# The last gate by TensorE with two more rows, in quarters; last embeddings in the row loop; last row scaled by VectorE

## The reference

```python
ffn = peer(x, peer_wq, peer_subkeys, peer_u, peer_v)    # 8 heads x 16 experts a position
x = layer_norm(DEEPNORM_ALPHA * x + ffn, ln2_g, ln2_b)
gate = sigmoid(x @ ple_wgate + ple_bgate)               # 1024 -> 1024
ple = gate * (p @ ple_wproj)                            # 256 -> 1024
x = layer_norm(DEEPNORM_ALPHA * x + ple, ln3_g, ln3_b)

def peer(x, w_q, sub_keys, u_tab, v_tab):
    q = (x @ w_q).reshape(B, S, 8, 2, 128)
    scores = einsum('bshpk,hpnk->bshpn', q, sub_keys)
    # top 16 of each half, top 16 of their 256 sums -> expert ids, softmax -> gates
    h = einsum('thkd,td->thk', u_tab[ids], x)
    act = gates * gelu(h)
    return einsum('thk,thkd->td', act, v_tab[ids])
```

## Time and profile before

| | us |
|---|---|
| median of 3 runs (lowest, highest) | 1508.1 (1507.87, 1511.52) |
| the profiled execution, its own time | 1511.14 |
| its span, first to last instruction | 1509.1 |
| busy: PE, DVE, ACT, POOL | 1156.4, 1071.6, 926.1, 587.5 |
| DMA in the chain that ended last | 32% |
| bytes moved, mean rate | 595.55 MB, 395 GB/s |

### The profile page before, as it was taken

How to read it: one execution, slowest core, us unless ns; L and a number is a source line. 1 busy time by engine, 2 the same in 40 slices (tenths; PEclk the granted TensorE clock), 3 DMA queues, 4 the chain that set the end, 5 groups by cost and what they waited for, 6 DMA issues and landing times.

```text
span 1509.1 us, 19032 instructions
## 1 busy us (share of the span) xinstructions
PE 1156.4 (77%) x6928; PEld 917.1 (61%) x6928; DVE 1071.6 (71%) x2604; ACT 926.1 (61%) x1577; POOL 587.5 (39%) x528
## 2 busy tenths in 40 slices
PE   8989999988666986777568977878566666677766
PEld 6556776666665775666546756555456665666553
DVE  0467776658777786778566666778976677789875
ACT  1136675667767787776556567665566666666561
POOL 1024444334444344344433444444345444534330
PEclk9999999989989999899777897999787777888898
DMA  9559999999999999999999999999999999999990
GB/s 370 208 232 421 421 420 422 420 421 421 421 421 421 394 394 422 421 421 420 424 421 421 399 421 422 419 422 420 402 422 421 420 421 420 422 379 404 407 387 21
DMA packets 84807, 595.55 MB, mean 395 GB/s; under 512 B 9445, under 2 KB 12005, under 8 KB 14826
## 3 DMA queue, kind: packets, MB, share of 16 engines
q0 software_dynamic: 73728, 536.90, 86.1%
q1 hardware_dynamic: 10986, 57.44, 9.4%
HBM read 592.21 MB, written 2.10 MB: 394 GB/s over the span
## 4 chain that ended last, share of the span: by engine, by line
DMA 32%; PE 24%; DVE 23%; ACT 11%; issue 5%; POOL 4%; SPq 0%; ACTq 0%; DVEq 0%
DMA arena<-in_uv,ids 32%; PE ps L844 10%; DVE arena L1251 9%; PE ps L634 4%; ACT arena L1008 4%; POOL arena L468 4%; PE ps L777 2%; PE ps L611 2%; PE ps L493 2%; PE ps L486 2%; ACT actv L1003 2%; DVE cands L1191 1%; DVE cands L1192 1%; DVE pick L1193 1%; PE ps L698 1%
## 5 line engine op out<-in xcount | busy, mean ns | idle before, releaser
L468 POOL DMA_INDIRECT arena<-in_uv,ids x512 | 582.4, 1137 | 834.3 <-PE ps L844 710.1
L844 PE MATMUL ps<-ident,arena 128*128 128x128 f32 x4096 | 631.9, 315 | 325.0 <-ACT arena L1008 323.6
L1251 DVE CUSTOM_DVE_ANT_0 arena<-arena 128x1024 f32<-128x1024 f32 x512 | 619.0, 1224 | 308.4 <-DMA arena<-in_uv,ids 301.2
L844 PEld LDWEIGHTS ps<-ident,arena 128*128 128x128 f32 x4096 | 549.4, 163 | 433.8 <-ACT arena L1008 395.0
L1008 ACT ACTIVATE arena<-arena,actv 128x1024 f32<-128x1024 f32 x512 | 556.9, 1135 | 0.0
L1000 ACT ACTIVATE gel<-hid 128x2 f32<-128x2 f32 x256 | 51.9, 203 | 448.3 <-DVE hid L1251 441.8
L634 PE MATMUL ps<-arena 128*128 128x128 f32 x1024 | 127.5, 286 | 0.8 <-ACT arena L934 0.8
L1003 ACT ACTIVATE actv<-gel,gates 128x1 f32<-128x1 f32 x512 | 122.9, 287 | 8.4
L634 PEld LDWEIGHTS ps<-arena 128*128 128x128 f32 x1024 | 126.0, 204 | 1.5 <-issue 1.5
L698 PE MATMUL ps<-arena 128*128 128x384 f32 x192 | 65.9, 486 | 0.0
L611 PE MATMUL ps<-arena 128*128 128x512 f32 x128 | 59.4, 610 | 1.1 <-DVE arena L1120 1.1
(11 more groups left out here) (141 smaller groups left out, 923.0 us busy)
## 6 DMA issues: line engine op xcount, KB each, us to landing
arena<-in_wq SPq DMA_DIRECT2D x22, 1024.0 KB
arena<-in_w_out SPq DMA_DIRECT2D x4, 2048.0 KB, 16.1
arena<-in_uv,ids POOLq DMA_INDIRECT x512
arena<-in_w_gate SPq DMA_DIRECT2D x1, 4096.0 KB, 17.9
arena<-in_w_k SPq DMA_DIRECT2D x4, 512.0 KB, 6.4
arena<-in_w_q SPq DMA_DIRECT2D x2, 1024.0 KB, 10.7
arena<-in_w_gv SPq DMA_DIRECT2D x1, 2048.0 KB, 16.1
arena<-in_w_v SPq DMA_DIRECT2D x1, 2048.0 KB, 21.6
```

The lines of the kernel that those rows point to most:

```text
L468: nc.gpsimd.indirect_dma_start(out=rows[:, c % RING, :], out_offset=None, in_=a["uv"][:, :], in_offset=bass.IndirectOffsetOnAxis(ap=ids[:, ...
L844: i = mm(ps[:, run_bank(r) + k // 4, (k % 4) * P:(k % 4 + 1) * P], rows[:, c % RING, D + k * P:D + (k + 1) * P], ident[:, :], is_transpose ...
L1251: v.tensor_tensor_reduce(out=r, in0=r, in1=x1[t], scale=1.0, scalar=0.0, op0=ALU.mult, op1=ALU.add, accum_out=hid[:, i, c:c + 1]).then_inc ...
```

## The change

The gate of a tile becomes sigmoid(rstd * (y @ W' - mu * sum(W') + sd * bias')), with sd = (var + eps) * rstd. The two corrections are one more matmul with two rows of weights (-mu and sd, `fixT`) against two rows (sum(W') and bias', `fix_rows`), accumulated onto the gate product. ACT reads PSUM and applies rstd as the sigmoid's scale, and `open_gate` goes. In detail:

- the two rows come from one set of matmuls with 2-column weights at steps 133 to 140; the 16 matmuls of the second set, a copy of 1024 columns and the addition of the bias go; one gain less is spread; the columns of gains are made at step 130 instead of 131, the gate weights scaled from 144 instead of 143;
- tile 0's tail begins at step 156 instead of 164;
- in a tail, PE transposes the two values at b+4 and adds the correction at b+7; sigmoids at b+8 instead of b+10; second embeddings at b+9 instead of b+8; DVE multiplies and adds at b+9 and b+11; variance at b+12 and norm at b+13, one step earlier;
- tile 3's embeddings run at step 250 in the loop;
- the last gathered row is scaled by DVE and not by ACT;
- tile 3's gate is made in four quarters of 256 columns.

```diff
-TAIL_AT = {0: 164, 2: 225, 1: 240}
+TAIL_AT = {0: 156, 2: 225, 1: 240}
-SPREAD_AT, COLUMNS_AT, BIAS_AT, SCALE_AT, MEAN_AT = 120, 131, 134, 143, 152
+SPREAD_AT, COLUMNS_AT, SUMS_AT, SCALE_AT = 120, 130, 133, 144
...
                 for k in range(k0, k0 + 2):
-                    w = neg_one[:, :] if i else gcols[:, KD + k:KD + k + 1].to_broadcast([P, P])
-                    m = mm(ps[:, 4 + j, :], w, w_gate[:, k, j * HALF:(j + 1) * HALF],
...
+                    mm(ps[0:2, 4 + j, :], gcols[:, k, :], w_gate[:, k, j * HALF:(j + 1) * HALF],
+                       start=(k == 0), stop=False, skip_group_check=True)
...
+            def transpose_fix(i, bank):
+
+                pe.wait_ge(fix_ready, i + 1)
+                if bank == 5:
+                    pe.wait_ge(y_read, i + 1)
+                nc.tensor.transpose(ps[0:2, bank, 0:P], fix[:, :], ident[:, :]).then_inc(fix_tr, 1)
+
+            def gate_fix(i, c0, c1, bank, place=0):
+
+                pe.wait_ge(fixT_ready, i + 1)
+                mm(ps[:, bank, place:place + c1 - c0], fixT[:, :], fix_rows[:, c0:c1], start=False, stop=True,
+                   skip_group_check=True).then_inc(gate_done, 1)
...
                     if step == b + 7:
+                        gate_fix(i, 0, HALF, 6)
+                        gate_fix(i, HALF, D, 4)
                         embedding_product(i, 0, 5)
-                    if step == b + 8:
-                        pe.wait_ge(gate_in, 2 * i + 1)
+                    if step == b + 9:
+                        pe.wait_ge(gate_ready, 2 * i + 1)
                         embedding_product(i, 1, 6)
+                if step == NU * NG - 6:
+                    pe.wait_ge(run_added, NR - 1)
+                    for j in range(2):
+                        embedding_product(NT - 1, j, 2 - run_bank(NR - 1) + j)
...
             y_transposes(last)
             pe.wait_ge(score_used, NU)
-            for j in range(2):
-                gate_product(last, j, 0, KD, 6 + j)
+            for c in range(4):
+                gate_product(last, c * QD, (c + 1) * QD, 0, KD, (6, 7, 4, 5)[c])
+                if c == 0:
+                    transpose_fix(last, run_bank(NR - 1))
+                else:
+                    gate_fix(last, (c - 1) * QD, c * QD, (6, 7, 4)[c - 1])
+            gate_fix(last, 3 * QD, D, 5)
...
+            def gate_sigmoid(i, n, c0, c1, bank):
+
+                act.wait_ge(gate_done, 2 * i + n + 1)
+                fn(gate[:, c0:c1], ps[:, bank, 0:c1 - c0], ACT.Sigmoid, scale=rstd[:, 0:1]).then_inc(gate_ready, 1)
...
+                if step == SUMS_AT + KD + 1:
+                    keep_sums()
                 for i in range(NT - 1):
                     b = TAIL_AT[TAILS[i]]
-                    if step == b + 10:
-                        gate_sigmoid(i, 0)
-                        gate_sigmoid(i, 1)
+                    if step == b + 6:
+                        keep_fix(i, 5)
+                    if step == b + 8:
+                        gate_sigmoid(i, 0, 0, HALF, 6)
+                        gate_sigmoid(i, 1, HALF, D, 4)
...
+            v.tensor_scalar(r, r, actv[:, (NU - 1) % 4, c:c + 1], None, ALU.mult).then_inc(last_scaled, 1)
             add_run(NR - 1)
```

More of the change, by code:

```diff
@@ L146, in build @@
         gG = sb("gG", [P, WB])
-        gcols = sb("gcols", [P, 2 * KD])
+        gcols = sb("gcols", [P, KD, 2])
         gaggr = sb("gaggr", [P, 2, 2])
         grstd = sb("grstd", [P, 2])
-        murs = sb("murs", [P, 1])
-        stats = sb("stats", [P, 2, 6])
+        fix = sb("fix", [P, 2])
+        fixT = sb("fixT", [2, P])
+        stats = sb("stats", [P, 4, 6])
         aggr = sb("aggr", [P, 2])
@@ L841, in combine @@
                     pe.wait_ge(run_added, r if r < 3 else r - 1)
-                pe.wait_ge(scaled, u * TOPK + c + 1)
+                if u * TOPK + c + 1 < NU * TOPK:
+                    pe.wait_ge(scaled, u * TOPK + c + 1)
+                else:
+                    pe.wait_ge(last_scaled, 1)
                 for k in range(KD):
@@ L1059, in _ @@
             last = NT - 1
-            gate_sigmoid(last, 0)
-            gate_sigmoid(last, 1)
+            keep_fix(last, run_bank(NR - 1))
+            for c in range(4):
+                gate_sigmoid(last, c, c * QD, (c + 1) * QD, (6, 7, 4, 5)[c])
         @block.vector
@@ L1317, in y_var @@
                 mean_var()
-                step(v.tensor_tensor(murs[:, :], aggr[:, 0:1], rstd[:, :], ALU.mult))
+                v.tensor_scalar(fix[:, 0:1], aggr[:, 0:1], -1.0, None, ALU.mult)
+                v.tensor_tensor(fix[:, 1:2], var_e[:, 0:1], rstd[:, 0:1], ALU.mult).then_inc(fix_ready, 1)
             def y_centre(i):
@@ L1328, in y_rescale, with add_embedding @@
                                             op0=ALU.mult, op1=ALU.add))
[L1330 to L1347 removed]
+            def add_embedding(i, n, c0, c1, bank, place, chunk):
+                part = gate[:, c0:c1]
+                dst = x2[TAILS[i]][:, c0:c1]
+                dve.wait_ge(gate_ready, 2 * i + n + 1)
+                if i < NT - 1:
+                    dve.wait_ge(embedding_done, 2 * i + n + 1)
+                else:
+                    dve.wait_ge(embedding_done, 2 * NT)
+                v.tensor_tensor(part, ps[:, bank, place:place + c1 - c0], part, ALU.mult).then_inc(ple_used, 1)
+                dve.wait_ge(ple_used, 2 * i + n + 1)
+                step(v.scalar_tensor_tensor(out=dst, in0=dst, scalar=ALPHA, in1=part, op0=ALU.mult, op1=ALU.add))
+                half_stats(dst, chunk)
             def background(at_step):
@@ L1421, in _ @@
             free = 2 - run_bank(NR - 1)
+            c = TOPK - 1
+            r = rows[:, c % RING, D:2 * D]
+            dve.wait_ge(actv_ready, NU * TOPK)
+            v.tensor_scalar(r, r, actv[:, (NU - 1) % 4, c:c + 1], None, ALU.mult).then_inc(last_scaled, 1)
             add_run(NR - 1)
@@ L1426, in _ @@
             y_rescale(last)
-            for j in range(2):
-                open_gate(last, j, 6 + j)
-                if j == 0:
-                    add_embedding(last, 0, free)
-            add_embedding(last, 1, free + 1)
-            mean_var()
+            for c in range(4):
+                add_embedding(last, c, c * QD, (c + 1) * QD, free + c // 2, c % 2 * QD, c)
+            mean_var(4)
             normed_halves(x2[TAILS[last]], ln3_g, ln3_b, out_ready)
```

131 lines of the change are left out of this document (51 added, 80 removed).

## The result

| | before | after |
|---|---|---|
| median of 6 runs (lowest, highest), us | 1508.8 (1507.87, 1511.52) | 1513.9 (1512.9, 1516.07) |
| ratio, 95% interval | | 1.0027 [1.0015, 1.004] |
| profiled execution, its span, clock | 1511.14, 1509.1, 0.878 | 1513.33, 1511.3, 0.879 |
| last dots end, last variance starts | 1472.92, 1501.14 | 1474.24, 1503.26 |

The kernel became 0.27% slower (4.1 us by the ratio of the runs side by side, 5.1 between the medians). By the bound of 0.3% this is no change, but it is outside the predicted range (1500 to 1510) and of the wrong sign. So the medians say how much, and the traces only where.

The account below looks back on a forecast made before the run. The stream of row gathers was taken to bound the loop, then the chain behind the last gather. Loop +0.2 and end -2.9 gave -2.7 us: 1508.4 profiled, 3.0 lower as median, 1505.4; range 1500 to 1510 (8 in 10).

Parts of the forecast that it names:

- Tile 2's tail: In the loop: PE's added matmuls and ACT's wait, less VectorE's lighter steps, cost +1.1 us; ends 0 and +4.5.
- Columns: In the loop: gain columns one step earlier, away from the query, win back 1.0 of the dip's 2.0 us.
- Tile 0's tail: In the loop, 8 steps earlier: VectorE's fewer, spread instructions give -0.6 of 1.6 us; ends -1.6 and +0.5.
- Dots: At the end: tile 1's norm moves out of the way of the last dots, -0.3 of 2.9 us.
- Last row by DVE: At the end: VectorE scales one row while ACT scales the other; -0.5 us taken, ends 0 and -1.1.
- Embeddings: At the end: 4.39 us leave the chain, but PE waits 0.7 for the last addition; net -3.7 us.
- Clock: At the end: the 8 transposes and 0.2 us of gate product now fall in the half-clock stretch, +1.0 us.
- Gate in quarters: Last tile's gate: 0.4 us wait for fix values, 0.1 small transpose, 1.72 for four fix matmuls; together +2.2 us.
- Behind PE: From PE's end to the last variance: 2.8 us where it was 4.51, -1.7; ends -1.2 and -1.9.
- ACT and PE hold each other up: Slower rival, tails of tiles 2 and 1: sigmoids waiting for PE block rows PE needs; 10.1 us in all, 1515.3; 13%.
- The clock stays low: Second rival, at the end: PE's idling misses the clock's rise, half speed under the gate product, +1.7 us, 1507.1; 17%.
- The fast rival: In the loop: the dips close, loop -3.0 us, with the end's -4.5 the time is 1500.6; 20%.

Follow-up runs that it names:

- e12: The changed kernel without the correction of the gate in any of the four tiles; ratio to the kernel before 0.9979.
- e10: The kernel before with columns at step 130, last embeddings at step 250, gate in quarters, last row by DVE, correction still by DVE; ratio 0.9982.
- e11: The changed kernel without the correction in the loop (tiles 0, 2 and 1), the last tile keeping it; ratio to the kernel before 0.9996.
- e7: The kernel before with only the last gathered row scaled by DVE; ratio to the kernel before 0.9993.
- e3: The kernel before with only the last tile's embeddings moved to step 250; ratio to the kernel before 0.9984.
- e1: The changed kernel with the last tile's embeddings again behind the loop; ratio to the kernel before 1.0029.
- e5: The changed kernel without the correction in the last tile; ratio to the kernel before 1.0001.
- e4: The changed kernel with three unused matmuls on PE ahead of the last step's rows; ratio to the kernel before 1.0006.
- e2: The changed kernel with the loop's sigmoids and what follows them later, last embeddings at step 252, PE's correction kept; ratio to the kernel before 1.0023.
- e8: The kernel before with only the columns of gains at step 130 instead of 131; ratio to the kernel before 0.9992.

## Why the prediction was wrong, step by step

**The step that failed** is the pricing of the correction by PE. It had three terms: +1.1 for tile 2's tail, +0.7 for tile 1's, and +2.2 for quarters and fix matmuls, 4.0 together, against -6.7 for all else. The runs put it at 7.2 us (the changed kernel against e12), and all else at -3.2 (e12 against the kernel before; e10 gives -2.7). Both halves were off: the cost by 3.2, the gains by 3.5. The correction's matmuls take 8.2 us of PE in the changed kernel's trace, three times 1.91 in the loop (from their start to that of the embeddings) and four times 0.62 at the end. I let the queue of gathers cover most of the loop's part and took none for tile 0; the runs charge it almost at its full length on PE.

- *Tile 2's tail*: ACT's wait was predicted at about 4.5 us with the table load in it, on the right rows, and it was 3.54 behind the load. The consequence was wrong. I wrote that "0.5 us is felt", because PE comes late too. But the region 1312 to 1384 lost 6.7 us where it had lost 5.0, +1.7, inside the ends of 0 and +4.5. That is about a quarter of the price I gave the rival in which PE and ACT hold each other up (2.7 of 10.1, with tile 1's tail). With tile 1's tail (3.7 lost, before 2.7: +1.0, predicted +0.7) the late tails cost 2.7 in the trace, predicted 1.8. The ratio of e11 says 4.7 us, give or take 2.5, for all three tails.
- *Columns*: the dip went wholly, better than the 1.0 taken, but the distance to the query, the reason given, is not what these traces show: the 32 matmuls ran mostly at full clock, 4.24 us and not 6.98. *Tile 0's tail*: its dip at 1060 went too. But neither gave a microsecond to the whole. Between 700 and 1312 seven kernels with the old loop lost 3.8 to 5.2 us, seven with the changed one 2.7 to 5.9. In place of the 1.9 us before 904 stand 2.3 us behind 1120 (in stretches the change does not touch), and in place of the dip at 1060 the one at 976. The predicted -1.6 was about 0: the step took a local repair for a gain. Why the later dips come is not settled.
- *Dots*: their end came 1.3 us later, at 1474.24, not 0.3 earlier. The last gather landed at 1472.99; I had worked out 1471.4 from the old landing. That is a part of the 2.7 us that the loop's windows lost more.
- *Last row by DVE*: 0.75 us for 1024 columns, not the 1.3 taken from the nearest row, and ready before ACT's row at 1476.03. The 16 transposes gave none of it back, as they ran at 1.2 GHz throughout (3.69). e7 alone measured -0.07 points (1 us), with an interval that includes both 0 and the predicted 0.5.
- *Embeddings*: the loop hid them, as predicted, except for a start of the next rows 1.8 us later. In the old kernel the move brings 0.16 points (e3), in an execution whose end ran at full clock throughout. In the changed kernel e1 shows no gain.
- *Clock*: +1.0 predicted. The stretch at 1.2 GHz lasted until after 1484. It cost 1.3 on the rows beyond the 2.36 I had for them, 0.2 on the transposes beyond what I had, and 1.1 under the first quarter, where I had 0.2. These are two thirds of what the end lost against its forecast. So the second rival, given 17% and 1.7 us, is what happened in this execution, and a little more. It is not the same in each: e3 had the level up from 1472, e5 from 1478. The Trainium skill ("TensorE: Matmul & The Clock Gate", Part 1) has the clock throttled by default and released by activity. The trace agrees in kind: PE idled 2.94 us before the rows and 0.88 us before the transposes, and rose only under the unbroken gate product. e4, with more activity, came out faster, by a difference at the edge of the noise.
- *Gate in quarters*: from its start to PE's end 17.34 us, less 1.1 of half clock 16.2; predicted 15.95. No wait for the fix values came (0.4 predicted), since they were there at 1486.19 and the slow first quarter ended at 1487.16; instead a fix matmul (two passes) took 0.62 (0.43 predicted) and the quarter behind one 3.65 where the second took 3.46.
- *Behind PE*: 3.35 us to the last variance, 2.8 predicted. The order closes the third quarter only behind the fourth's product. So ACT took both sigmoids in a row from 1499.94, and DVE had six instructions behind them, 0.46 us from start to start, 2.76 us. In e12, where the third quarter is closed early, it is 1.96.

The last step I took, to set the changed kernel 3.0 us under its profile because the old one stood so, was luck of one execution. It made the forecast of 1505.4 out of 1508.4; the 35 runs of the kernel before in one batch range from 1506.65 to 1515.21.

The rivals: "ACT and PE hold each other up" had the right place and sign, and PE as the full engine, but put too much on it (1515.3; it was to be decided from 2.9 us, and the loop's windows lost 2.7 more). Its mutual wait is there in the trace, 3.54 and 1.19 us, but e2 does not show that it costs. "The clock stays low" came true beside it in the profiled execution. The fast rival had right that two dips close, and wrong that this shortens the loop.

What stays open: 2.0 us of loss between 1120 and 1312 that five of the seven kernels with the changed loop show (1.1 to 2.7) and none of the seven with the old (0.2 to 0.6); how the loop's share divides between PE's added matmuls and ACT's wait; and how much of e4's 0.21 points is the clock and how much is noise, since one trace a kernel was taken.

## What to carry to other kernels

Work moved from an engine beside the path (in the loop, DVE with its two instructions a half) to the engine that everything queues behind (PE) is to be priced at its full length there: here 8.2 us of matmuls cost about 7.2, where the forecast counted on cover and took 4.0. Whoever waits for it now also waits in PE's order, with its own queue behind it; whether that costs more is not shown here. A dip in the transfers that is closed pays only if the rate behind it stays full: compare the loss over the whole loop, not the window. And a dip can come from the clock's level in that stretch and go without any edit, as in e7. Last, take the parts of a change apart before judging it: here four of them together made the kernel 0.18 points faster, and one took more than that back.

## What the runs showed of the hardware

The correction's matmul has two rows of weights, and is no cheaper for it. In the loop a pair of 512 columns took 1.98 us, as long as the pair of the embeddings behind it with 128 rows (1.98). In the last tile it cost more. The tensor engine's weight loads there, in the changed kernel:

```profile
1487.00 3.32 PEld L777 LDWEIGHTS ps<-arena 128*128 128x128 f32 x16
1490.65 0.29 PEld L790 LDWEIGHTS ps<-arena,fixT 2*128 2x128 f32 x2 [0.33 <-issue]
1491.28 3.32 PEld L777 LDWEIGHTS ps<-arena 128*128 128x128 f32 x16 [0.33 <-issue]
```

Two passes take 0.62 us in the chain where two of the gate product take 0.43, and each time the kind of weights changes, from 128 rows to 2 and back, the load idles 0.33 us (`issue`). Within a quarter the sixteen loads run as one group with no such gap.

VectorE's multiplication of 1024 columns by one value a row, SBUF to SBUF, took 0.75 us, and two additions of 512 columns from PSUM 1.29. The instructions of 256 columns took 0.42 to 0.43.

```profile
1475.03 0.75 DVE L1445 TENSOR_SCALAR arena<-arena,actv 128x1024 f32<-128x1024 f32 x1 [0.78 <-ACT actv L1028]
```

The same 32 matmuls of the columns took 6.98 us at a granted clock of 0.50 and 3.88 us where it was 0.95 and 0.90 (e7). At the end of the kernel the level differed from execution to execution, also with the same code there: full from 1480 on in the kernel before, from 1474 on in e8.
